# A fourth section of a decoder block's projection run before its shift is known

## What is computed

```
mod = silu(c) @ w_ada + b_ada                 -> shift1, scale1, gate1, shift2, scale2, gate2
h   = rms_norm(x, g_norm1) * (1 + scale1) + shift1
proj = h @ w_in     # gq gk gv gg ga_low | fq fk fv f_logit | gate_a gate_b
o_a = gated linear attention (gq, gk, gv, decay), normalised, * silu(gg)
o_b = forgetting attention (fq, fk, fv, f_logit)
merged = sigmoid(gate_a) * (o_a @ w_proj_gla) + sigmoid(gate_b) * (o_b @ w_proj_fox)
x = x + gate1 * (merged @ w_out)
h2 = rms_norm(x, g_norm2) * (1 + scale2) + shift2
x = x + gate2 * (relu(h2 @ w_ff1) ** 2 @ w_ff2);   out = rms_norm(x, g_final)
```

## Time and profile before

| what | value |
|---|---|
| median of 3 runs | 1865.07 us (1863.80 to 1866.28) |
| the profiled execution's own time | 1863.37 us |
| its span, first to last instruction | 1861.6 us, mean granted TensorE clock 0.992 |
| TensorE busy | 1826.9 us, 98% of the span |
| weight loads into TensorE | 1485.3 us, 80% |
| VectorE / ScalarE / GpSimd busy | 1250.1 / 851.6 / 32.7 us |
| read from HBM | 442.12 MB, 239 GB/s over the span |

### The profile page before, as it was taken

The page is one execution under the profiler, slowest core; times in us unless marked ns, Lnnn a source line. Parts: engine busy times, 40 slices in busy tenths (PEclk is TensorE's granted clock), DMA queues, the critical chain, the costliest instruction groups (busy, mean ns, idle before and its releaser), DMA issues.

```text
span 1861.6 us, 21801 instructions
## 1 busy us (share of the span) xinstructions
PE 1826.9 (98%) x8353; PEld 1485.3 (80%) x8353; DVE 1250.1 (67%) x1402; ACT 851.6 (46%) x1089; POOL 32.7 (2%) x60
## 2 busy tenths in 40 slices
PE   6999999999999999999999999999999999999998
PEld 3667888888888888888888888788888888888886
DVE  5997667676666667667766787876555555555555
ACT  4445555455544554334444455443444344434443
POOL 1011000000000000000000000000000000000000
PEclk8999999999999999999999999999999999999999
DMA  9998898899997987999999786787666666666663
GB/s 382 401 338 245 214 229 279 245 236 252 208 209 248 211 249 238 251 272 308 332 258 273 270 274 216 229 276 229 191 186 189 193 191 182 192 193 192 183 191 124
DMA packets 213329, 445.72 MB, mean 239 GB/s; under 512 B 14693, under 2 KB 31429, under 8 KB 212842
## 3 DMA queue, kind: packets, MB, share of 16 engines
q1 hardware_dynamic: 211320, 440.51, 79.4%
q10 hardware_dynamic: 1138, 3.50, 0.5%
q0 software_dynamic: 768, 0.31, 0.2%
HBM read 442.12 MB, written 2.10 MB: 239 GB/s over the span
## 4 chain that ended last, share of the span: by engine, by line
PE 89%; DVE 1%; issue 1%; ACT 1%; DMA 0%; ACTq 0%; POOLq 0%; POOL 0%; DVEq 0%
PE ps L1817 83%; PE ps L1801 1%; PE ps L1921 1%; DVE wlo L1195 0%; PE ps L1973 0%; DMA raw<-in_w_in 0%; PE ps L1727 0%; PE ps L1725 0%; ACT whi L716 0%; PE ps L1930 0%; PE ps L2068 0%; PE ps L1856 0%; PE ps L1869 0%; PE ps L1943 0%; PE ps L1944 0%
## 5 line engine op out<-in xcount | busy, mean ns | idle before, releaser
L1195 DVE TENSOR_TENSOR wlo<-raw,whi 128x1024 fp32r<-128x1024 f32 x604 | 738.4, 1224 | 551.8 <-ACT whi L716 548.8
L716 ACT ACTIVATE whi<-raw 128x1024 fp32r<-128x1024 f32 x604 | 639.2, 1059 | 914.5 <-PE ps L1817 638.6
L1817 PE MATMUL ps<-whi,hT 128*128 128x512 f32 x3264 | 1042.9, 396 | 4.0 <-DVE wlo L1195 3.8
L1817 PEld LDWEIGHTS ps<-whi,hT 128*128 128x128 f32 x3264 | 616.3, 189 | 148.8 <-issue 11.1
L1817 PE MATMUL ps<-wlo,hT 128*128 128x512 f32 x1632 | 638.0, 391 | 0.0
L1817 PE MATMUL ps<-whi,oaT 128*128 128x512 f32 x1248 | 390.6, 391 | 0.0
L1817 PEld LDWEIGHTS ps<-wlo,hT 128*128 128x128 f32 x1632 | 308.6, 189 | 63.8 <-issue 1.9
L1817 PEld LDWEIGHTS ps<-whi,oaT 128*128 128x128 f32 x1248 | 234.3, 188 | 49.5 <-issue 1.2
L1817 PE MATMUL ps<-wlo,oaT 128*128 128x512 f32 x624 | 242.9, 389 | 0.0
L1313 DVE SCALAR_TENSOR_TENSOR acc<-raw,cond,acc 128x1024 f32<-128x1024 f32 x120 | 153.3, 1278 | 0.2
L1817 PEld LDWEIGHTS ps<-wlo,oaT 128*128 128x128 f32 x624 | 117.2, 188 | 25.2 <-issue 1.2
(11 more groups left out here) (247 smaller groups left out, 825.7 us busy)
## 6 DMA issues: line engine op xcount, KB each, us to landing
raw<-in_w_ff SPq DMA_DIRECT2D x264, 512.0 KB, 4.2
raw<-in_w_in SPq DMA_DIRECT2D x248, 512.0 KB, 7.1
raw<-in_w_ada SPq DMA_DIRECT2D x128, 512.0 KB, 5.8
first<-in_w_ada SPq DMA_DIRECT2D x64, 512.0 KB, 10.1
raw<-in_w_in SPq DMA_DIRECT2D x64, 256.0 KB, 6.2
raw<-in_w_proj_fox SPq DMA_DIRECT2D x32, 512.0 KB, 5.6
raw<-in_w_proj_gla SPq DMA_DIRECT2D x32, 512.0 KB, 5.4
raw<-in_w_out SPq DMA_DIRECT2D x32, 512.0 KB, 5.5
```

The source lines that it names most:

```text
L716: nc.scalar.activation(parts(g)[0][:], raw[POS_G[g] % RING][:], ACT.Copy).then_inc(s_hi, 1)
L1195: V.tensor_tensor(rest[:], raw[POS_G[g] % RING][:], top[:].bitcast(F32), ALU.subtract).then_inc(s_lo, 1)
L1817: i = T.matmul(ps[bank(name, t)][:], src[:, kt, hl, tk], w[:, k, :], start=(kt == 0 and n == 0), stop=(kt == KT - 1 and n == 2))
```

## The change

The section gb 0 moves from the head of MIX to the end of the early sections, as `EARLY`. It is multiplied with h without the shift, ACT copies its result from PSUM to a new tile `gbh`, its weights ride along a second time in GLA's first and second round (units 142 to 163, every third), DVE adds their products with shift1 up in a new tile `accb`, and at unit 167 a fourth sum goes into `gz`, on which ACT later applies the sigmoid. FOX and GLA stand 8 units later than before (G_FOX is 32, G_GLA is 128), and OUT and FF where they stood. 35 units are loaded and 34 multiplied among the pieces of w_ada, by a denser `LOAD_AT`; the first three units' loads all come behind piece 15. `shift_lo` stands at pieces 55 to 62 instead of 49 to 56, since gb 0 still reads h without the shift. Head 3 begins in GLA's third round at its unit 19. Rides of kind "a" in GLA and MIX come every 2 and 3 units in turn, where in GLA they came every 3.

```diff
+EARLY = [("gb", 0)]
-MIX = [(what, it) for it in range(4) for what in ("gb", "ob", "ga", "oa")]
+MIX = [(what, it) for it in range(4) for what in ("gb", "ob", "ga", "oa") if (what, it) not in EARLY]
-NAME = HEAD + FOX + GLA + MIX + OUT + FF
+NAME = HEAD + EARLY + FOX + GLA + MIX + OUT + FF
...
-LOAD_AT = [13, 14, 15] + [17 + 7 * _i // 4 for _i in range(9)] + [32] + [33 + 2 * _i for _i in range(1, 12)] + [57, 59, 61]
+LOAD_AT = [15, 15, 15] + [17 + 7 * _i // 4 for _i in range(9)] + [32] + [33 + 4 * _i // 3 for _i in range(22)]
+SHIFT_P = 55
...
+SHIFT_GB = [G_GLA + 14 + 3 * n for n in range(UG)]
+SHIFT_AT = {G_FOX + 22: 0, SHIFT_GB[-1] + 4: 3}
...
-        g += 5 if g < 43 else 2 if g < G_GLA or g >= UP_FROM else 3 if g < G_MIX or n % 2 else 2
+        g += 5 if g < G_FOX + 19 else 2 if g < G_GLA or g >= UP_FROM or n % 2 else 3
...
-                act.wait_ge(s_pe, UNIT[HEAD[-1], kt // KU] + 1)
+                act.wait_ge(s_pe, UNIT[EARLY[-1], kt // KU] + 1)
...
+                    if it == 0 and u == 2:
+
+                        act.wait_ge(s_hl, 2 * KT)
+                        take(("gb", 0), tok(gbh), ACT.Copy)
...
-                    act.wait_ge(s_e, 12)
+                    act.wait_ge(s_wadd, 4)
+                    nc.scalar.activation(gz[:], gz[:], ACT.Sigmoid).then_inc(s_gz0, 1)
+                    return
...
-                if P_0[3] < p <= P_0[3] + 8:
-                    shift_lo(p - P_0[3] - 1)
+                if SHIFT_P <= p < SHIFT_P + 8:
+                    shift_lo(p - SHIFT_P)
...
+                if j == SHIFTS:
+
+                    dve.wait_ge(s_pt, FH)
...
                 elif j >= SHIFTS:
-                    dve.wait_ge(s_mod, ADA0 + 2)
-                    rows = [(up0[:], r[:, k, :], KU * (j - SHIFTS) + k, 1) for k in range(KU)]
+                    rows = [(accb[:], r[:, k, :], KU * (j - SHIFTS) + k, 1) for k in range(KU)]
...
                 if n == 3:
 
-                    V.tensor_scalar(up0[:], ps[7][:], 1.0, None, ALU.mult).then_inc(s_wadd, 1)
+                    dve.wait_ge(s_e, 6)
+                    for t in range(TT):
+                        dve.wait_ge(s_bk[bank(("gb", 0), t)], emptied(("gb", 0)))
+                        i = V.tensor_tensor(gz[:, t, :], gbh[:, t, :], ps[7][:], ALU.add)
+                    i.then_inc(s_wadd, 1)
...
+                if h == 1:
+                    dve.wait_ge(s_wadd, 4)
...
+                    if it == 3:
+                        gla_head(3, u - 19)
```

More of the change, by code:

```diff
@@ L52 @@
 G_OUT = G_MIX + UG * len(MIX)
+MIX_0 = G_MIX - UG * len(EARLY)
 G_FF = G_OUT + UG * len(OUT)
@@ L130 @@
 SHIFTS = KT + UG
[L131 to L134, removed]
+GB_SHIFTS = SHIFTS + UG
+UP_SHIFTS = GB_SHIFTS + UG
+SHIFT_Q = [G_FOX + n for n in (1, 3, 6, 8, 11, 13, 16, 18)]
+SHIFT_GB = [G_GLA + 14 + 3 * n for n in range(UG)]
+SHIFT_AT = {G_FOX + 22: 0, SHIFT_GB[-1] + 4: 3}
+UP_FROM = MIX_0 + 34
 def mods_before(m):
@@ L163, in ride_all @@
         RIDE_AT[g] = ("w", j)
-    g, m, k, j, n, free = 28, 0, 0, UG, 0, 0
+    for j, g in enumerate(SHIFT_GB):
+        RIDE_AT[g] = ("w", SHIFTS + j)
+    g, m, k, j, n, free = G_FOX + 4, 0, 0, UG, 0, 0
     while m < 6:
+        if g in SHIFT_GB:
+            g += 1
         if G_FOX + 24 <= g and j < SHIFTS and (n % 2 == 0 or g < free) or \
-                UP_FROM <= g and SHIFTS <= j < UP_SHIFTS and (n % 3 == 0 or g < free):
+                UP_FROM <= g and GB_SHIFTS <= j < UP_SHIFTS and (n % 3 == 0 or g < free):
             RIDE_AT[g] = ("w", j)
@@ L578, in load @@
                     parts = source(what if kind == "g" else UNIT[("fq", 0), what] if what < UG
-                                   else UNIT[("up", 0), what - SHIFTS])
+                                   else UNIT[("gb", 0), what - SHIFTS] if what < GB_SHIFTS
+                                   else UNIT[("up", 0), what - GB_SHIFTS])
                     n = NB // len(parts)
@@ L915, in _ @@
                     hi(12 + kt // 4 - 2)
-            for g in range(14, 27):
+            for g in range(14, G_FOX + LEAD):
                 hi(g)
@@ L920, in _ @@
                         norm1_scale(kt)
-                if 19 <= g < 23:
-                    for kt in (2 * (g - 19), 2 * (g - 19) + 1):
+                if 28 <= g < 32:
+                    for kt in (2 * (g - 28), 2 * (g - 28) + 1):
                         shift_hi(kt)
@@ L997, in _ @@
             for it in range(4):
-                for u in range(32):
-                    hi(G_MIX + 32 * it + u + LEAD)
-                    if u == 0 and not it:
+                for u in range(0 if it else UG, 32):
+                    hi(MIX_0 + 32 * it + u + LEAD)
+                    if u == UG and not it:
                         gla_stage(4, 0)
@@ L1247, in shift_piece @@
                     dve.wait_ge(s_bt, 4)
+                if j == SHIFTS:
+                    dve.wait_ge(s_pt, FH)
                 if j < UG:
                     rows = [(accq[:], r[:, k, :], KU * j + k, 1) for k in range(KU)]
+                elif j >= GB_SHIFTS:
+                    dve.wait_ge(s_mod, ADA0 + 2)
+                    rows = [(up0[:], r[:, k, :], KU * (j - GB_SHIFTS) + k, 1) for k in range(KU)]
                 elif j >= SHIFTS:
-                    dve.wait_ge(s_mod, ADA0 + 2)
-                    rows = [(up0[:], r[:, k, :], KU * (j - SHIFTS) + k, 1) for k in range(KU)]
+                    rows = [(accb[:], r[:, k, :], KU * (j - SHIFTS) + k, 1) for k in range(KU)]
                 else:
@@ L1531, in gated @@
                 gates = ("gb" if what == "ob" else "ga", it)
+                if gates in EARLY:
+                    dve.wait_ge(s_gz0, 1)
                 for t in range(TT):
                     bank_done(dve, name, t)
-                    dve.wait_ge(s_bk[bank(gates, t)], emptied(gates))
+                    if gates not in EARLY:
+                        dve.wait_ge(s_bk[bank(gates, t)], emptied(gates))
                     dst = mtok[:, t, cols] if what == "ob" else mt[:, t, :]
@@ L1549, in _ @@
             for it in range(4):
-                for u in range(32):
-                    g = G_MIX + 32 * it + u
+                for u in range(0 if it else UG, 32):
+                    g = MIX_0 + 32 * it + u
                     lo(g + LEAD)
@@ L1741, in shift_sum @@
                 if n:
-                    i = T.matmul(ps[7][:], ones[:], up0[:] if n == 3 else accv[:, n - 1, :], start=True, stop=True)
+                    i = T.matmul(ps[7][:], ones[:], (accv[:, 0, :], accv[:, 1, :], accb[:], up0[:])[n - 1], start=True, stop=True)
                 else:
@@ L2072, in _ @@
             for it in range(4):
-                for u in range(32):
-                    mod(G_MIX + 32 * it + u)
-                    shift_sum(G_MIX + 32 * it + u)
+                for u in range(0 if it else UG, 32):
+                    mod(MIX_0 + 32 * it + u)
+                    shift_sum(MIX_0 + 32 * it + u)
                     if not it:
```

17 lines of the change are left out of this document (12 added, 5 removed).

## The result

The changed kernel takes 1875.18 us (median of five executions, 1873.17 to 1877.35), the kernel before 1865.07 us (five, 1863.8 to 1867.15). The ratio is 1.0050, with a 95% interval of 1.0039 to 1.0061. I had forecast 1858.3 us: the sign was wrong, and the time lies outside the range. The profiled execution's span is 1872.7 us against 1861.6.

What follows compares the result with a forecast made beforehand. TensorE, busy 98% of the span, was taken as the bound, so only its waits could be won: -8.1 - 1.5 + 0.9 + 2.0 = -6.7, giving 1856.7, or 1858.3 us as median; range 1853 to 1867.

Steps and rivals of the forecast that it cites:

- The start: From unit 10 to the fourth sum: TensorE becomes the bound and lost waits come back, 8.1 us gained, bounds 4 to 9.8.
- so with the delay of the first loads they have landed by about 138 us: Loads up to the fourth sum: 54.0 MB at 401 GB/s take 135 us, landing before TensorE wants the last ones.
- the start falls short: Rival, chance 0.12: at the start engines wait for each other in circles of four or five buffers; half the gain, 1862.4 us.
- unit 13's wait: At the start, TensorE's wait for unit 13's low part, 2.74 us before, was to shrink to 1.3 us.
- The 0.7 us that the first loads behind piece 15 should bring: At the start, pieces 14 and 15 come forward, so VectorE's copy no longer waits 0.70 us for the first sum.
- The copy: TensorE's 2.69 us stop for ScalarE's copy of fq 0 at 153.6 us shrinks; 1.5 us gained, between 0 and 3.5.
- The sum: One more sum of 512 columns on TensorE costs 0.86 us, all of it on the path.
- GLA: Eight rides, 4.2 MB of loads and 1.53 us of VectorE each, lose 2.0 us in GLA; bounds 0 and 14.9.
- given back in GLA: Rival, chance 0.16: each of six rides costs 1.8 us of load time, 9.8 us lost in GLA, 1866.2 us in all.
- The sentence from the Trainium skill: GLA's rides: a 435 GB/s DMA ceiling, full rate from 512 bytes, leaves room at 192 GB/s, so they cost 0.
- MIX: From unit 200 to the end, the forecast loss was 0.
- Head 3: Moves with gb 0, first steps beside gv 3: nothing taken, at worst one wait well below 1 us.

Runs made afterwards that it cites:

- pieces_ahead: Against the changed kernel, SyncE issues two more w_ada pieces ahead of each unit's load from the thirteenth on; ratio to before 1.0021.
- tiny_loads: Changed kernel with the gate's eight rides loading only 32 of 512 columns, VectorE doing all its work on them; ratio to before 1.0010.
- late_rides: Changed kernel with the gate's eight rides at units 158 to 179 instead of 142 to 163, MIX's later rides where they stood before; ratio to before 1.0014.
- one_ride: Changed kernel with only the first of the gate's eight rides kept, places of all other rides and sums kept; ratio to before 1.0010.
- after_again: The changed kernel profiled a second time, nothing edited; by the unit-by-unit table its end is 8.2 us later than the first profile of before.
- light_adds: Changed kernel with the gate's rides loaded whole, but VectorE working on 16 of 512 columns from the second ride on; ratio to before 1.0044.

## Why the prediction was wrong

**The start, -8.1 forecast.** At the fourth sum 0.9 us was gained in the first profile and 3.5 in the second (136.03 + 21.8 us less 156.93 and 154.30). The step that failed is "so with the delay of the first loads they have landed by about 138 us". It divides bytes by 401 GB/s, as if loads only wait for the DMA engines, and the last piece landed at 154.5 us. Loads also wait in SyncE's queue, behind loads that have no buffer yet. Two more pieces ahead brought the last piece to 146.7 us and were worth some 2.7 us at the sum. The rate was too high as well: 401 GB/s is one window of before, and in the windows of pieces_ahead above it is 352 and 351. The rival "the start falls short" named the circle of buffers, but priced it at half the gain and did not see that the pieces hang in it.

The count of work on TensorE was right in the main: unit 13's wait was 1.57 us for 1.3, the gain at unit 20 was 6.0 us, and once the pieces come in time the sum is 2.7 us from the forecast place. Of these, 1.6 us are seven pieces at 1.18 us each: I had read 0.95 from the begin of a piece to the begin of the next unit, and left out the gap before the piece and the slower unit behind it. The 0.7 us that the first loads behind piece 15 should bring can't be seen: unit 10 begins at 75.58 and 74.63 us in the two profiles, and at 74.84 and 75.27 before.

**The copy, -1.5 forecast.** Nothing came: 2.67 us of wait are left. I argued that the load has less ahead of it than before, and none of the nine profiles with the copy in its old place and the change bears that out (2.1 to 3.0 us of wait, even in pieces_ahead, where the pieces were over sooner); why the load is no faster stays open. The mechanism, a copy queued behind a high part whose load is late, was right, and its whole price of 3.5 us lies within what the edit of the order gave (3.2 and 4.5).

**The sum, +0.86.** It was as forecast: at 605.45 us, 0.86 us on the path of TensorE.

**GLA, +2.0 forecast.** Measured 5.9 and 5.5 without the sum (5.0 to 8.3 in the four other profiles with these rides whole). It lies in the range that I gave the term, 0 to 14.9, but the reason that drew it to the low end was wrong. I compared rates over 40 us and looked for the thinnest unit. The loss is made for the most part at one place, where the head's products, a ride and a low part follow one another on VectorE, and I had not written down that sequence. The rival "given back in GLA" priced 9.8, and 5.9 lies midway between that and the forecast; its mechanism, the bytes, is the one that tiny_loads bears out, but through the time until one load lands and not through a full rate. The sentence from the Trainium skill, page "DMA: Bandwidth & Descriptors", section Specifications, by which this term would be 0, does not hold here: with the rides' loads cut to 1/16 the loss falls by 4 us, though the changed kernel moved only 263 GB/s from 560 to 600 us, at a share of 0.88.

**MIX, nothing forecast.** Measured 5.3 and 5.1, of which 0.7 is within what before loses itself. The step missing is that a plan computed in one loop moves every later ride when one is added: the rides of MIX stand one unit earlier (what was at 230 is at 229, and so on), and I took that for nothing without looking at the slack there. How much of the loss that makes stays open: late_rides, with the places of before, lost 5.6.

**Head 3.** Nothing forecast, and nothing measured beside the sum (one_ride).

By the table: forecast -6.7, measured +11.1 in the first profile, 17.8 us apart. 8.6 of it are the start and the copy, 3.9 GLA, 5.3 MIX. It is not a single large error. In the start a rate stood in for a queue; in GLA, and it seems in MIX, cover was measured as an average and used up at a point.

## What to carry to other kernels

Bytes over a rate is the time of a load only if it can be issued: follow the queue that issues it, and ask what stands ahead and which ring that waits for. When work moves ahead of a load-bound stretch, put the urgent loads ahead of the ones that can wait, and copies that need no load ahead of those that do; each of two such edits took about half of the changed kernel's loss of 0.50% away (1.0021 and 1.0025), and with the rides later as well it became a gain of 0.11%. Work that rides along is priced at the place where it meets other work in the same engine's order, not by the mean share.

## What the runs showed of the hardware

The loads of w_in run at very different rates at the same full share, and the rates go with which block of 512 columns they read. Three stretches of the kernel before, of ga 1, ga 2 and ga 3, whose units and rides are alike (columns as in the earlier trace rows):

```profile
815.00:835.00 20.00, 20.00 (x90) 16.57 (x89) 11.93 (x13) 5.88 (x6) 0.00 (x0) 1.00 0.99 256
900.00:920.00 20.00, 20.00 (x88) 16.20 (x87) 15.65 (x15) 7.43 (x7) 0.00 (x0) 1.00 0.96 332
990.00:1010.00 20.00, 20.00 (x90) 16.57 (x89) 10.76 (x10) 5.97 (x6) 0.00 (x0) 1.00 1.02 247
```

ga 2 moves 332 GB/s, ga 1 and ga 3 move 256 and 247, at shares of 0.96 to 1.02. In the trace the packets of 2 KB take about 100 ns in the sections with an even block and 150 to 195 ns in the odd ones. It is in these odd sections that MIX loses its time (ga 1 and ga 3, above). That the block is the cause is read from where the slow packets stand, not shown by an edit. Why they are slow no run here shows.

And the clock: one execution of the kernel before was granted 0.52 for about 6 us at 184 us where another was granted 1.00 for the same instructions. A difference of 3 us between two single profiles can be this alone. In both, the 17-row matmuls of the decay (L1869) stood right before. Behind a wait of TensorE for the mask in GLA the clock differed too: after 2.85 us of standing 0.69 was granted over the next 5.5 us, after 2.3 us 0.67 over 5.1 us (after_again), and after 1.6 and 1.5 us 1.00 (tiny_loads, light_adds).
